# One decoder block on one core: the experts' rows packed in halves of 64, two halves per step

## The chip, the core and the metric

The kernel runs on one core of one Trainium2 chip. The metric is the device time of one launch in microseconds (us), the median over several executions. A profiled execution adds a trace, in which PE is TensorE's matmuls, PEld its weight loads, DVE is VectorE, ACT is ScalarE, POOL is GpSimd and SP is SyncE; a q behind a name (SPq) is that engine's instruction queue, where DMA issues and register work stand.

## The reference, cut to what matters

The block has a mixer (a projection, an SSD scan, attention, an output projection) and then a mixture of 32 experts. The change touches only the experts and the routing that prepares them. There are 1024 tokens of 1024 numbers, and each token goes to 2 experts of one group of 8:

```python
g_w, g_idx = lax.top_k(g_prob, 1)                 # one of 4 groups
e_w, e_idx = lax.top_k(e_prob, MOE_TOP_K)         # 2 of its 8 experts
w = g_w * e_w / sum(e_w)
gate = t @ w_gate[e]; up = t @ w_up[e]            # 1024 -> 256 each, float32
out += (silu(gate) * up * w) @ w_down[e]          # 256 -> 1024
```

So 2048 rows (token, expert) have to be computed. An expert's weights are three matrices of 1 MB, 3 MB in all. How many rows each expert gets follows from the reference and its inputs: for experts 0 to 31 it is 36, 106, 61, 55, 73, 31, 78, 86, 38, 33, 68, 47, 37, 26, 14, 63, 34, 45, 97, 50, 49, 133, 49, 97, 46, 191, 64, 121, 40, 69, 53, 58. Two experts have more than 128 rows. In pieces of at most 64 rows they are 45 pieces: 1 2 1 1 2 1 2 2 1 1 2 1 1 1 1 1 1 1 2 1 1 3 1 2 1 3 1 2 1 2 1 1.

## The kernel before

Everything is written by hand, with its own queue for each engine and counters (semaphores) between them. The work before the experts fills about 760 us: projection, scan, attention, output projection with residual, norm and router logits. Then a chain of small VectorE operations (lines 1497 to 1583) turns the router's choice into places: for each row of each tile the token that is to be gathered (`idx_i`) and the row to which the result goes (`dst_i`).

**Tiles.** Every expert has one tile of 128 rows, and rows beyond 128 go to extra tiles, two of them in straight code (`MORE`) and more in a branch that is taken only if needed. That makes 34 tiles (`TILES`), tile n for expert n, tiles 32 and 33 for the two experts over 128 rows. The last block of the program runs them; its functions are called `four` on each engine.

**One tile on TensorE**, in this order in its queue: `gate_up` of tile n (8 float32 matmuls with a stationary piece of `xg_T`, 128x128, and 512 moving columns, gate and up side by side; the profile counts a float32 matmul as two instructions, so 16), `tokens` of tile n+1 (8 transposes of the gathered rows `x_g`), `down` of tile n-1 (4 matmuls, 8 instructions) and `hidden_T` of tile n (2 transposes). ScalarE and VectorE copy the transposes into `xg_T` (`tx`), make SiLU(gate) and its product with up (`silu`, `gated`), and copy the results into `y_e` (`y_of`). GpSimd issues the gather of the rows and the scatter of the results (`gather`, `scatter_of`), after a copy of the index column (`idx_now`, `dst_now`).

**Weights.** `load_expert` on SyncE issues three DMAs of 1 MB into one of four slots (`RING` is 4). Tile n uses slot n mod 4. Experts 0 to 3 are loaded while the routing runs. From then on SyncE waits until `down` of the tile that last used the slot is done, and loads the next expert into it: the counter `dn_done` is raised by `down`.

**After the tiles** the results are read back from DRAM (`y_g`), weighted, summed, normed and stored; that part stays.

Of the kernel before, what the change touches and what calls it, by code (L numbers as in the profile page):

```python
# [7 lines left out]
F32 = mybir.dt.float32  # L8
# [6 lines left out]
P = 128  # L15
# [11 lines left out]
def hybrid_block(nc, x, c, positions, ada_w, ada_b, pre_norm_mix, post_norm_mix, pre_norm_ffn,  # L27
# [36 lines left out]
    with ctx:  # L64
# [18 lines left out]
        causal_b = keep("causal_b", [P, P], BF16)  # L83
        G1 = keep("G1", [P, D])
# [35 lines left out]
        XT = 16  # L120
        assert XT * (P + 1) > 2 * T - P
        NTILE = E + XT
# [4 lines left out]
        META = XT + 1  # L127
        meta_i = keep("meta_i", [P, META], I32)
# [80 lines left out]
        rt = [place(f"rt{i}", R_A + 81920 + 1024 * i, [P, NT, E]) for i in range(8)]  # L209
        oh1, oh2, lm, cand, both, rank, over, lm2 = rt  # L210
        oh1, oh2, lm, cand, both, rank, over, lm2 = (t[:, :, :] for t in rt)
# [3 lines left out]
        cmp = place("cmp", R_U + 3072, [P, XT, E])[:, :, :]  # L215
        cmp_n = place("cmp_n", R_U + 5120, [P, E, NT])[:, :, :]
# [5 lines left out]
        cnt, n_over, incl, base_t, lo128, dlt, zero32 = (tiny(f"tinyc{i}", 11 + i, [P, E])[:, :] for i in range(7))  # L222
# [5 lines left out]
        thr = tiny("thr", 23, [P, NT])[:, :]  # L228
        meta_f = tiny("meta_f", 24, [P, META])[:, :]
# [6 lines left out]
        W_OFF = [R_A + 32768, R_S, R_A, R_A + 57344]  # L236
        w_gu = [place(f"w_gu{i}", o, [P, 2, KC, FF]) for i, o in enumerate(W_OFF)]
        w_dn = [place(f"w_dn{i}", o + 16384, [P, FC, D]) for i, o in enumerate(W_OFF)]
        x_g = [place(f"x_g{i}", R_Z + 4096 * i, [P, D]) for i in range(2)]
        xg_T = [place(f"xg_T{i}", R_Z + 8192 + 4096 * i, [P, KC, P]) for i in range(2)]  # L240
        y_e = [place(f"y_e{i}", R_U + 4096 * i, [P, D]) for i in range(2)]
# [3 lines left out]
        idx_now = [place(f"idx_now{i}", R_A + 88064 + 32 * i, [P, 1], I32) for i in range(2)]  # L245
        dst_now = [place(f"dst_now{i}", R_A + 88128 + 32 * i, [P, 1], I32) for i in range(2)]
# [6 lines left out]
        w_diag = place("w_diag", R_U + 8192, [P, 2 * len(PE_TILES), P])  # L253
# [8 lines left out]
        def pe_sum(t):  # L262
# [15 lines left out]
            idx_read route_act wgu_loaded0 wgu_loaded1 wgu_loaded2 wgu_loaded3 wdn_loaded0 wdn_loaded1  # L278
            wdn_loaded2 wdn_loaded3             pool_step dve_step""".split()
# [3 lines left out]
            ye_stored1 v_gu0 v_gu1 v_dn0 v_dn1 v_xg0 v_xg1 v_idx v_tx v_txa v_txd v_gud v_silu v_hid v_th v_thr gathers_begun  # L283
            idx_step xg_loaded0 xg_loaded1 ya_scaled ysum_done ysum_sq o_scaled o_done o_stored yg_loaded0 yg_loaded1 yg_loaded2
            yg_loaded3 yg_loaded4 yg_loaded5 yg_loaded6 yg_loaded7 moe_stored w_diag ysum_pe dst_step v_stored v_down v_ya v_yd""".split()
# [992 lines left out]
        def load_expert(eng, e, r, gu, dn):  # L1278

            one = lambda v: v[bass.ds(e, 1), :, :, :].rearrange("a p k f -> (a p) k f")  # L1280
            eng.dma_start(w_gu[r][:, 0, :, :], one(wg_v)).then_inc(gu, 16)
            eng.dma_start(w_gu[r][:, 1, :, :], one(wu_v)).then_inc(gu, 16)
            eng.dma_start(w_dn[r][:, :, :], one(wd_v)).then_inc(dn, 16)

        EB = NG

        with nc.Block() as block:

            @block.sync
            def _(sp):  # L1290
# [10 lines left out]
                load_expert(sp, 0, 0, S["wgu_loaded0"], S["wdn_loaded0"])  # L1301
# [6 lines left out]
                load_expert(sp, 2, 2, S["wgu_loaded2"], S["wdn_loaded2"])  # L1308
                sp.wait_ge(S["x2_done"], NT)
                load_expert(sp, 3, 3, S["wgu_loaded3"], S["wdn_loaded3"])  # L1310
                sp.wait_ge(S["lg_done"], NT)
                load_expert(sp, 1, 1, S["wgu_loaded1"], S["wdn_loaded1"])
# [4 lines left out]
            @block.gpsimd  # L1317
            def _(pool):
                for t in range(NT):
                    inverse_root(pool, 5, t, S["yo_sq"], t + 1)  # L1320
                    inverse_root(pool, 6, t, S["x2_sq"], t + 1)

# [107 lines left out]
            def _(dve):  # L1430
# [98 lines left out]
                for j in range(2):  # L1529
                    dve.tensor_scalar(place_p[:, j:j + 1], tok_id[:, 0:1], 2.0, float(1 + j), ALU.mult, ALU.add)  # L1530
                dve.tensor_scalar(place_t, iota_row[:, 0:NT], 2.0 * P, None, ALU.mult)
                link(dve.tensor_scalar(thr, iota_row[:, 1:NT + 1], float(P), None, ALU.mult))
                dve.tensor_scalar(lo128, iota_row[:, 0:E], float(P), None, ALU.mult)
                dve.wait_ge(S["ranks_done"], 1)
                link(dve.tensor_copy(cnt, BANK[2][:, 0:E]))

                link(dve.tensor_tensor(cmp_n, cnt.unsqueeze(2).to_broadcast([P, E, NT]),
                                       thr.unsqueeze(1).to_broadcast([P, E, NT]), ALU.is_gt))
                link(dve.tensor_reduce(n_over, cmp_n, AX_X, ALU.add))
                link(dve.tensor_tensor_scan(incl, n_over, zero32, 0.0, ALU.add, ALU.add))  # L1540
                link(dve.tensor_tensor(base_t, incl, n_over, ALU.subtract))
                link(dve.tensor_scalar(base_t, base_t, float(E - 1), float(P), ALU.add, ALU.mult))
                link(dve.tensor_tensor(dlt, base_t, lo128, ALU.subtract))
                ex = lambda v: v.unsqueeze(1).to_broadcast([P, NT, E])
                rk = BANK[1][:, 0:NT * E].rearrange("p (t e) -> p t e", e=E)
                link(dve.tensor_scalar(over, rk, float(P), None, ALU.is_ge))
                link(dve.tensor_tensor(over, over, ex(dlt), ALU.mult))
                link(dve.tensor_tensor(rank, rk, over, ALU.add))
                link(dve.tensor_tensor(rank, rank, ex(lo128), ALU.add))
# [11 lines left out]
                for j in range(2):  # L1561
# [5 lines left out]
                    if j == 0:  # L1567
# [3 lines left out]
                link(dve.tensor_tensor(cmp, iota_row[:, 0:XT].unsqueeze(2).to_broadcast([P, XT, E]),  # L1571
                                       incl.unsqueeze(1).to_broadcast([P, XT, E]), ALU.is_ge))
                link(dve.tensor_reduce(meta_f[:, 0:XT], cmp, AX_X, ALU.add))
                link(dve.tensor_scalar(meta_f[:, 0:XT], meta_f[:, 0:XT], float(E - 1), None, ALU.min))
                link(dve.tensor_copy(meta_f[:, XT:], incl[:, E - 1:E]))
                dve.tensor_copy(meta_i[:, :], meta_f)
# [7 lines left out]
                dve.wait_ge(S["idx_read"], 1)  # L1584


        RING = 4
        assert E % RING == 0 and E > RING
        MORE = 2
        TILES = E + MORE  # L1590
        LATER_CREDIT = {"v_down": 2}

        with nc.Block() as block:  # L1593
            def rounds(eng, four):

                four(0, range(RING), True, False)
                with eng.Fori(1, E // RING - 1) as i:
                    four(i * RING, range(RING), False, False)
                four(E - RING, range(RING + MORE), False, True)

            def extra(eng, one):

                n_extra = eng.snap(eng.value_load(meta_i[0:1, XT:XT + 1], min_val=0, max_val=XT))
                with eng.If(n_extra > MORE):
                    with eng.Fori(MORE // 2, XT // 2) as i:
                        for u in range(2):
                            one(i, u)
# [3 lines left out]
            def _(sp):  # L1611
                def four(n0, us, first, last):
                    for u in us:
                        if first:
                            continue
# [358 lines left out]
```

## Time and profile before

| what | value |
|---|---|
| median of 3 executions | 1243.04 us (1242.4 to 1243.77) |
| profiled execution, its own time | 1242.94 us |
| its span, first to last instruction | 1240.3 us |
| granted TensorE clock, mean | 0.938 of full speed |
| PE busy in the span | 1061.1 us (86%) |
| from the first `gate_up` to the end of the last `down` | 800.91 to 1192.58 us |

The span is the time between the first and the last instruction of the trace; 2.6 us lie around it. A stretch of the trace is read by its granted clock first (1.00 is 2.4 GHz, 0.50 is 1.2 GHz), then by who waits for whom. "Idle before" in a row is the time in which an engine did nothing ahead of an instruction, with what ended it.

### The profile page before, as it was taken

Reading aid. Unit: us, or ns where it says so; the run is one execution under the profiler, and the core shown is the slowest. Engines: PE = TensorE matmul, PEld = TensorE weight load, DVE = VectorE, ACT = ScalarE, POOL = GpSimd, SP = SyncE. Lnnn points to the kernel's source line nnn. Section 1 sums busy time; section 2 is a strip of 40 time slices with the busy share of each in tenths; the row PEclk is TensorE's granted clock in tenths of the full one; section 3 lists DMA queues with packets and bytes.
Section 4 is the critical chain, followed back from the end, with each engine's and each line's share of the span. In section 5 each row is a group of like instructions: output and inputs, shape, how many; then the busy total and the mean of one; then the engine's idle time right before and its main releaser. Section 6 shows DMA issues by size and latency. Waiting matters only on the chain. (4 is left out here: it accounts for less than half of the span.)

```text
span 1240.3 us, 11686 instructions
## 1 busy us (share of the span) xinstructions
PE 1061.1 (86%) x4040; PEld 591.2 (48%) x4040; DVE 506.4 (41%) x825; ACT 260.0 (21%) x585; POOL 210.0 (17%) x324
## 2 busy tenths in 40 slices
PE   1499999996989999787699994399999999999954
PEld 1444444443455666587345553244445445444521
DVE  4543437345656555588143345511121112112217
ACT  1420001213444344233022211011111111111113
POOL 5100000223200000046210000112221221222114
PEclk9989999997999999898699996599999999999977
DMA  9763332000000000300401216238887878988537
GB/s 334 260 261 136 136 136 42 1 1 0 1 1 1 1 1 1 135 2 1 141 35 68 68 51 241 107 131 344 305 313 307 319 302 322 348 323 320 211 135 290
DMA packets 46355, 190.05 MB, mean 153 GB/s; under 512 B 17314, under 2 KB 18402, under 8 KB 29026
## 3 DMA queue, kind: packets, MB, share of 16 engines
q1 hardware_dynamic: 34596, 166.80, 35.8%
q0 software_dynamic: 10672, 18.45, 4.2%
q10 hardware_dynamic: 1040, 4.19, 0.9%
q8 instruction: 27, 0.44, 0.1%
q14 instruction: 20, 0.16, 0.0%
HBM read 182.07 MB, written 26.21 MB: 168 GB/s over the span
## 5 line engine op out<-in xcount | busy, mean ns | idle before, releaser
L1715 PE MATMUL PS<-w_gu,xg_T 128*128 128x512 f32 x544 | 241.5, 597 | 1.1 <-ACT xg_T L1800 1.1
L1715 PEld LDWEIGHTS PS<-w_gu,xg_T 128*128 128x128 f32 x544 | 101.8, 192 | 116.8 <-issue 115.2
L1726 PE MATMUL PS<-w_dn,hid_T 128*128 128x512 f32 x272 | 122.5, 593 | 0.9 <-DVE hid_T L1878 0.9
L1344 PE MATMUL PS<-w_out_sb,cat_T 128*128 128x512 f32 x256 | 113.5, 602 | 2.8 <-ACT cat_T L1400 2.8
L673 PE MATMUL PS<-hT,w_in_sb 128*128 128x512 f32 x256 | 112.2, 601 | 0.0
L1875 DVE TENSOR_TENSOR hid<-PS,hid_s 128x256 f32<-128x256 f32 x34 | 14.4, 425 | 224.2 <-ACT hid_s L1803 224.2
L361 POOL TENSOR_SCALAR rstd<-stat 128x1 f32<-128x1 f32 (+1 forms) x48 | 21.9, 456 | 408.1 <-ACT junk L468 206.3
L991 PE MATMUL PS<-kT,qT 96*128 96x512 f32 (+4 forms) x192 | 76.6, 509 | 3.0 <-ACT qT L782 3.0
L673 PEld LDWEIGHTS PS<-hT,w_in_sb 128*128 128x128 f32 x256 | 49.4, 193 | 62.1 <-issue 62.1
L1344 PEld LDWEIGHTS PS<-w_out_sb,cat_T 128*128 128x128 f32 x256 | 48.7, 193 | 62.0 <-issue 58.4
L876 DVE TENSOR_REDUCE row_max<-PS 128x1 f32<-128x1024 f32 (+7 forms) x64 | 48.2, 754 | 63.8 <-PE PS L993 63.7
L1726 PEld LDWEIGHTS PS<-w_dn,hid_T 128*128 128x128 f32 x272 | 49.2, 190 | 50.3 <-issue 49.3
L794 ACT ACTIVATE probs<-PS,row_max 128x1024 f32<-128x1024 f32 (+7 forms) x64 | 47.5, 742 | 97.8 <-DVE row_max L876 97.4
L1881 DVE COPY y_e<-PS 128x512 f32<-128x512 f32 x34 | 23.5, 692 | 95.6 <-PE PS L1726 95.6
L1803 ACT ACTIVATE hid_s<-PS 128x256 f32<-128x256 f32 x34 | 13.1, 385 | 222.5 <-PE PS L1715 222.5
L683 PE MATMUL PS<-w_in_sb,hT 128*128 128x512 f32 x128 | 56.2, 592 | 0.0
L1003 PE MATMUL PS<-ident,probs 128*128 128x128 f32 x288 | 43.4, 278 | 12.4 <-ACT probsT L802 6.9
L1657 POOL COPY dst_now<-dst_i 128x1 int32 (+1 forms) x34 | 6.2, 183 | 248.7 <-DVE y_e L1881 149.2
L1710 PEld LDWEIGHTS PS<-ident,x_g 128*128 128x128 f32 x272 | 35.9, 190 | 23.8 <-issue 15.9
L692 PE MATMUL PS<-w_in_sb,hT 128*128 128x424 f32 x128 | 46.9, 519 | 0.0
L635 PE MATMUL PS<-ident,xn 128*128 128x128 f32 x64 | 14.5, 404 | 36.7 <-DVE xn L490 36.7
L1003 PEld LDWEIGHTS PS<-ident,probs 128*128 128x128 f32 x288 | 30.9, 141 | 29.4 <-ACT probs L794 24.1
(318 smaller groups left out, 1441.1 us busy)
## 6 DMA issues: line engine op xcount, KB each, us to landing
w_gu<-in_w_gate_dram SPq DMA_DIRECT2D x34, 1024.0 KB, 4.9
w_gu<-in_w_up_dram SPq DMA_DIRECT2D x34, 1024.0 KB, 7.5
w_dn<-in_w_down_dram SPq DMA_DIRECT2D x34, 1024.0 KB, 10.6
ada_later<-in_ada_w_dram SPq DMA_DIRECT2D x16, 1024.0 KB, 4.9
ada_first<-in_ada_w_dram SPq DMA_DIRECT2D x8, 1024.0 KB, 12.6
y_g<-y_rows SPq DMA_DIRECT2D x8, 1024.0 KB, 11.8
x_in<-in_x_dram SPq DMA_DIRECT2D x8, 512.0 KB, 3.7
w_in_sb<-in_w_in_dram ACTq DMA_DIRECT2D x1, 4096.0 KB, 13.2
```

What stands on the lines that cost most here:

```text
L673: last = pe.matmul(BANK[4 + n % 4][:, :], w_in_sb[:, k, XC0 + ct * P:XC0 + (ct + 1) * P], hT[:, k, hh * HALF:(hh + 1) * HALF], start=(k == ...
L683: last = pe.matmul(BANK[t % 2][:, 0:IN_SSD], hT[:, k, t * P:(t + 1) * P], w_in_sb[:, k, 0:IN_SSD], start=(k == 0), stop=(k == KC - 1))
L692: last = pe.matmul(BANK[6 + t % 2][:, 0:REST], hT[:, k, t * P:(t + 1) * P], w_in_sb[:, k, XC1:], start=(k == 0), stop=(k == KC - 1))
L794: act.activation(probs[b][:, 0:n], PS[:, 2 * b:2 * b + 2, :].rearrange("p a n -> p (a n)")[:, 0:n], ACT.Exp, bias=row_max[:, b:b + 1], acc ...
L876: dve.tensor_reduce(row_max[:, b:b + 1], PS[:, 2 * b:2 * b + 2, :].rearrange("p a n -> p (a n)")[:, 0:n], AX_X, ALU.max, negate=True).then ...
L991: pe.matmul(BANK[2 * b + c0 // HALF][:, 0:c1 - c0], qT[h][0:depth(h), i * P:(i + 1) * P], kT[h][0:depth(h), c0:c1], start=True, stop=c1 < ...
L1003: last = pe.transpose(BANK[4 + j // 4][:, j % 4 * P:(j % 4 + 1) * P], probs[g % 2][:, j * P:(j + 1) * P], ident[:, :])
L1344: last = pe.matmul(BANK[2 + t % 2 * 2 + j], cat_T[t % 2][:, k, :], w_out_sb[:, k, j * HALF:(j + 1) * HALF], start=(k == 0), stop=(k == KC ...
L1710: last = pe.transpose(BANK[k // 4][:, k % 4 * P:(k % 4 + 1) * P], x_g[u][:, k::KC], ident[:, :])
L1715: last = pe.matmul(BANK[bank], xg_T[b][:, k, :], w_gu[r][:, :, k, :], start=(k == 0), stop=(k == KC - 1))
L1726: last = pe.matmul(BANK[5 + j], hid_T[b][:, k, :], w_dn[r][:, k, j * HALF:(j + 1) * HALF], start=(k == 0), stop=(k == FC - 1))
L1881: return dve.tensor_copy(y_e[b][:, HALF:], BANK[6])
```

## The change

Experts' rows are laid out in halves of 64 rows, one behind the other, each expert with at least one half. A step takes two consecutive halves, whatever experts they belong to: the first in rows 0 to 63, the second in rows 64 to 127. For each piece of the contraction TensorE gets two matmuls with 64 stationary columns, one for each half, which write PSUM partitions 0 to 63 and 64 to 127, and each has its own expert's weights as the moving operand. There are 23 steps in straight code (`STEPS`) and 9 more in a branch.

- The ring still has four slots of 3 MB. Where a step's experts lie is read from a small table (`pair_i`) into a register (`slot_of`). The first half's matmuls read the ring by that register.
- The second half's weights are copied first from the ring to a fixed place: `near_gu` (ScalarE its gate part, VectorE its up part, 128x2048 each) and `near_dn` (one 128x1024 each). There is one such buffer. ScalarE reads four more numbers from the table, how far each slot must have been loaded, and waits for the loads (`nearer`).
- SyncE reads from a table (`free_i`) after which step the slot of expert e-4 is free, waits for that `down`, and loads expert e. Nobody else waits for loads.
- The routing chain is shorter in front (no `cmp_n`, `over`, `cmp`), with 32 columns for 48, and a new chain of about 17 small VectorE operations makes the two tables at the start of the last block. The first two gathers are issued at the end of the block before it, and gathers and scatters take their indices without the copy.

The core of the diff; the functions of before that it removes are printed above:

```diff
-        XT = 16
-        NTILE = E + XT
+        HT = P // 2
+        RING = 4
+        NTILE = (E + 2 * T // HT) // 2
...
+        near_gu = place("near_gu", R_Z + 8192, [P, 2, KC * FF])
+        near_dn = [nc.alloc_sbuf_tensor_at("near_dn0", [P, D], F32, offset=SPENT + 8192), place("near_dn1", R_U + 8192, [P, D])]
...
+        STEPS = 23
...
             def _(sp):
+                sp.wait_ge(S["pairs_made"], 1)
+                for e in range(RING, E):
+                    r = e % RING
+                    used = sp.value_load(free_i[0:1, e - RING:e - RING + 1], min_val=1, max_val=NTILE)
+                    sp.wait_ge(S["dn_done"], used)
+                    load_expert(sp, e, r)
...
+                def gate_up(n, w):
...
+                    pe.wait_ge(S["near_gu_act"], n + 1)
+                    pe.wait_ge(S["near_gu_dve"], n + 1)
...
                     for k in range(KC):
+                        for u in range(2):
+                            rows_ = slice(u * HT, (u + 1) * HT)
+                            last = pe.matmul(BANK[2 + b][rows_, :], xg_T[b][:, k, rows_], gu[u][:, :, k, :],
+                                             start=(k == 0), stop=(k == KC - 1))
...
+                def run(lo, hi):
...
+                    for n in range(lo, hi):
+                        gate_up(n, now)
...
+                        if n + 1 < hi:
+                            now = pair(n + 1)
+                            tokens_T(n + 1)
+                        if n > lo:
+                            down(n - 1, was)
+                        hidden_T(n)
+                    down(hi - 1, before_)
...
+                def nearer(n):
+                    w = slot_of(act, 2 * n + 1)
+                    landed = [act.value_load(pair_i[2 * n + 1:2 * n + 2, 1 + r:2 + r], min_val=3 * 16, max_val=3 * 16 * E // RING)
+                              for r in range(RING)]
+                    for r in range(RING):
+                        act.wait_ge(S[f"w_loaded{r}"], landed[r])
+                    act.sem_inc(S["w_here"], 1)
+                    act.activation(near_gu[:, 0, :], w[:, 0 * KC * FF:1 * KC * FF], ACT.Copy).then_inc(S["near_gu_act"], 1)
...
+                        silu(n)
+                        if n + 1 < hi:
+                            nxt = nearer(n + 1)
+                            tx(n + 1)
+                        if n > lo:
+                            y_of(n - 1)
+                        nearer_down(n, now)
```

TensorE's queue before, one tile in the loop (line 1715 is `gate_up`, 1710 the transposes of the gathered rows, 1726 `down`, 1720 `hidden_T`):

```order
L1715 MATMUL PS<-w_gu_257,xg_T_267 128x512 x8
L1710 MATMUL PS<-ident,x_g_264 128x128 x8
L1726 MATMUL PS<-w_dn_260,hid_T_274 128x512 x4
L1720 MATMUL PS<-ident,hid_273 128x128 x2
L1715 MATMUL PS<-w_gu_258,xg_T_266 128x512 x8
```

TensorE's queue now, from the last matmuls of a `gate_up` (line 1678) to the first of the next one (1658 are the transposes of rows, 1703 `down`, 1687 `hidden_T`; TENSOR_LOAD is the register load, ISA register work):

```order
L1678 MATMUL PS<-ring,xg_T_263 64x512
L1678 MATMUL PS<-near_gu,xg_T_263 64x512
L1602 TENSOR_LOAD pair_i
L1602 ISA x2
L1658 MATMUL PS<-ident,x_g_262 128x128 x8
L1703 ISA
L1703 MATMUL PS<-ring,hid_T_275 64x512
L1703 MATMUL PS<-near_dn_268,hid_T_275 64x512
...
L1687 MATMUL PS<-ident,hid_272 128x128 x2
L1678 ISA
L1678 MATMUL PS<-ring,xg_T_264 64x512
L1678 MATMUL PS<-near_gu,xg_T_264 64x512
```

The order of the four groups is the one of before; each full matmul has become a pair of 64 columns with register work ahead, and `down` of step n-1 still stands between `gate_up` of n and of n+1.

ScalarE's queue before, one tile (1803 `silu`, 1800 `tx`, 1806 `y_of`):

```order
L1803 ACTIVATE hid_s_270<-PS 128x256
L1800 ACTIVATE xg_T_267<-PS 128x512
L1806 ACTIVATE y_e_269<-PS 128x512
```

ScalarE's queue now, one step from `silu` (1754) on. Row 1602 is the register with the slot, the four loads of 1765 say how far the slots must be loaded (the rows here are two of the four), 1770 waits for that and copies, 1746 is `tx`, 1761 `y_of`, 1776 the copy for `down`:

```order
L1754 ACTIVATE hid_s_271<-PS 128x256
L1602 TENSOR_LOAD pair_i
L1602 ISA x2
L1765 TENSOR_LOAD pair_i
L1765 ISA x2
L1765 TENSOR_LOAD pair_i
L1765 ISA x2
...
L1770 ISA
L1770 ACTIVATE near_gu<-ring 128x2048
L1746 ACTIVATE xg_T_264<-PS 128x512
L1761 ACTIVATE y_e_266<-PS 128x512
L1776 ISA
L1776 ACTIVATE near_dn_268<-ring 128x1024
```

Five register loads and the copy into `near_gu`, with its wait for the loads, have moved in between `silu` of a step and `tx` of the next one.

## Rows read from the trace of the kernel before

**Rows 1.** Page, granted clock and DMA share in 40 slices

```profile
PEclk9989999997999999898699996599999999999977
DMA  9763332000000000300401216238887878988537
```

**Rows 2.** Chain that ended last: start, length, engine, line, count

```profile
1029.08 6.87 PE PS L1715 x16
1036.83 3.44 PE PS L1726 x8
1040.49 6.87 PE PS L1715 x16
...
1188.87 3.71 PE PS L1726 x8
```

**Rows 3.** Waits on SyncE's queue, 800 to 1200 us: total, times, longest

```profile
SPq L1281 <- PE PS L1726: 296.8, 28, 30.9
```

**Rows 4.** Page, DMA issue of an expert's third matrix: median to landing

```profile
w_dn<-in_w_down_dram SPq DMA_DIRECT2D x34, 1024.0 KB, 10.6
```

**Rows 5.** Windows: busy per engine, granted clock, DMA share, GB/s

```profile
770.00:772.00 2.00, 0.00 (x0) 0.00 (x0) 1.86 (x5) 0.00 (x0) 0.00 (x0) 0.50 1.01 426
1000.00:1100.00 100.00, 100.00 (x301) 49.81 (x301) 19.07 (x36) 14.22 (x27) 20.17 (x34) 1.00 0.86 327
```

**Rows 6.** DMA queues, 790 to 1200 us: packets, MB, share of 16

```profile
q0 software_dynamic: 9792, 16.80, 11.0%
```

**Rows 7.** Timeline around a load of tiles: `down` end, SyncE's issues

```profile
1131.61 0.33 SPq L1281 DMA_DIRECT2D w_gu<-in_w_gate_dram  x1
1131.61 0.60 ACT L1806 ACTIVATE y_e<-PS 128x512 f32<-128x512 f32 x1 [2.84 <-PE PS L1726]
...
1143.03 0.60 ACT L1806 ACTIVATE y_e<-PS 128x512 f32<-128x512 f32 x1 [2.84 <-PE PS L1726]
...
1143.97 0.35 SPq L1281 DMA_DIRECT2D w_gu<-in_w_gate_dram  x1
...
1144.89 0.38 SPq L1283 DMA_DIRECT2D w_dn<-in_w_down_dram  x1
```

**Rows 8.** Timeline of TensorE in attention, 501 to 511 us

```profile
502.00 1.31 PE L1016 MATMUL PS<-probsT,v_sb 128*64 128x128 f32 x20
503.25 0.91 PE L991 MATMUL PS<-kT,qT 96*128 96x384 f32 x2
...
509.70 0.88 PE L1016 MATMUL PS<-probsT,v_sb 128*64 128x128 f32 x12
510.51 0.49 PE L991 MATMUL PS<-kT,qT 96*128 96x128 f32 x2
```

**Rows 9.** Groups by form: copies on ScalarE and VectorE, mean ns

```profile
L1800 ACT ACTIVATE xg_T<-PS 128x512 f32<-128x512 f32 x34 | 20.3, 598 | 43.4 <-PE PS L1710 43.4
L1421 ACT ACTIVATE junk<-x 128x1024 f32<-128x1024 f32 x8 | 8.5, 1058 | 28.6 <-DVE x L1478 28.6
L501 DVE TENSOR_SCALAR acc<-ada_later,c_act 128x2048 f32<-128x2048 f32 x2 | 2.6, 1278 | 0.0
```

**Rows 10.** Timeline, start of the expert stage

```profile
798.11 1.97 PE L1710 MATMUL PS<-ident,x_g 128*128 128x128 f32 x8 [7.67 <-DMA x_g<-h_rows,idx_now]
800.91 9.37 PE L1715 MATMUL PS<-w_gu,xg_T 128*128 128x512 f32 x16 [0.83 <-ACT xg_T L1800]
```

**Rows 11.** Windows of 1 us after it (clock is the third last)

```profile
804.00:805.00 1.00, 1.00 (x2) 0.34 (x1) 0.00 (x0) 0.00 (x0) 0.00 (x0) 0.50 0.36 147
806.00:807.00 1.00, 1.00 (x3) 0.40 (x3) 0.00 (x0) 0.00 (x0) 0.00 (x0) 1.00 0.00 0
```

**Rows 12.** Timeline of VectorE in the routing, then the first gather

```profile
779.09 0.42 DVE L1546 TENSOR_SCALAR rt<-PS 128x256 f32<-128x256 f32 x1
...
791.69 0.19 DVE L1583 TENSOR_SCALAR idx_i<-dst_i 128x48 int32<-128x48 int32 x1
...
793.87 1.19 POOL L1651 DMA_INDIRECT x_g<-h_rows,idx_now  x1 [0.98 <-POOL idx_now L1648]
```

More of the change, by code:

```diff
@@ L1583, in _, with steps, slot_of @@
                 dve.tensor_scalar(idx_i[:, :], dst_i[:, :], 1, None, ALU.logical_shift_right).then_inc(S["idx_read"], 1)
[L1584 to L1591, printed above, removed]
-        with nc.Block() as block:
[L1594 to L1607, printed above, removed]
+        with nc.Block() as block:
+            def steps(eng, run):
+                run(0, STEPS)
+                n_steps = eng.snap(eng.value_load(free_i[0:1, E - 1:E], min_val=1, max_val=NTILE))
+                with eng.If(n_steps > STEPS):
+                    run(STEPS, NTILE)
+            def slot_of(eng, m):
+                a = eng.value_load(pair_i[m:m + 1, 0:1], min_val=0, max_val=max(W_OFF) // (4 * UNIT))
+                return ring[:, bass.ds(a, SLOT), :].rearrange("p a b -> p (a b)")
@@ L1664, in scatter_of, with scatter @@
[L1664 to L1665 removed]
+                def scatter(n):
+                    b = n % 2
                     pool.wait_ge(S["ye_act"], n + 1)
                     pool.wait_ge(S["ye_dve"], n + 1)
[L1668 to L1680 removed]
@@ L1781, in _ @@
-                pe.wait_ge(S["ye_act"], TILES)
-                pe.wait_ge(S["ye_dve"], TILES)
-                extra(pe, one)
+                            for u in range(2):
+                                rows_ = slice(u * HT, (u + 1) * HT)
+                                last = pe.matmul(BANK[5 + j][rows_, :], hid_T[b][:, k, rows_],
+                                                 (near_dn[k] if u else far[:, k, :])[:, j * HALF:(j + 1) * HALF], start=(k == 0), stop=(k == FC - 1))
+                    last.then_inc(S["dn_done"], 1)
@@ new lines, in run @@
+                def run(lo, hi):
+                    tokens_T(lo)
+                    if lo == 0:
+                        pe.wait_ge(S["pairs_made"], 1)
+                    now = pair(lo)
+                    for n in range(lo, hi):
+                        gate_up(n, now)
+                        if n > lo:
+                            was = before_
+                        before_ = now
+                        if n + 1 < hi:
[5 more added lines that the diff above has]
+                    down(hi - 1, before_)
```

464 lines of the change are left out of this document (202 added, 262 removed).

## The prediction

> **What bounds the kernel now.** I read the granted clock first: full speed through the slices of the expert stage [rows 1], so matmul times there are at 2.4 GHz. Then the chain that ended last. From 801 to 1193 us it is TensorE alone, tile after tile: 6.87 us of `gate_up`, 3.44 of `down`, the transposes between, and the next `gate_up` starts 11.41 us after the last one [rows 2]. Nothing waits for weights: it is SyncE that waits for TensorE, 28 times, 296.8 us in all [rows 3]. That wait is what the reader should keep in mind, because it is the reserve. A slot is freed by `down` of tile n and needed again by `gate_up` of tile n+4, three tiles or 30 us later, and the load takes about 11.5. Last, the DMA share: 0.86 of 16 engines, 327 GB/s, in a stretch of full work [rows 5], so the transfers are close behind TensorE. 34 tiles of 11.41 are 388 us; with the cold start the stage takes 391.7.
>
> **The step on TensorE.** 45 halves make 23 steps in place of 34 tiles. Does a pair of 64-column matmuls cost one full matmul? The attention already does this: two heads write the two halves of the partitions in turn. 20 such instructions of 128 columns take 1.31 us and 12 take 0.88 [rows 8], so one more costs (1.31-0.88)/8 = 54 ns. A full matmul instruction of 512 columns costs 6.87/16 = 429 ns [rows 2], which is 107 ns for 128. The pair runs at full overlap, and I take a step's `gate_up` as 6.87 and `down` as 3.44. The bounds are 1.0 and 2.0 times that; the second is excluded by these rows except for what is new here, a register-addressed operand and register work ahead of each pair. I keep 1.3 as the upper end.
>
> At one place a rule and the rows have to be weighed. The next instructions after the 20 start at 503.25, 1.25 us after 502.00, where 20 x 54 ns is 1.08; after the 12 it is 0.81 against 0.65 [rows 8]. So a change between pairs and full matmuls seems to cost about 0.17 us. There are four in a step. Two of them (into the transposes, into `down`) lie before the release of a slot; in the steps that wait for weights, 11 by the count below, they are on the path: 11 x 0.35 = 4 us. The Trainium skill, TensorEngine Tiling (Array Packing), Key Properties, says that a change of tiling mode drains TensorE. It gives no time; by the rule alone all 92 changes would count, 92 x 0.17 = 16 us, an estimate, by these rows the sum has 4.
>
> **The chain on ScalarE.** After `gate_up` of n, ScalarE must do `silu`, five register loads, the copy into `near_gu` and `tx` before `gate_up` of n+1. A register load is in the trace only on SyncE: for tile 32's weights the first issue comes 0.94 us after the copy that starts at the same `down` end, without a load 0.00 [rows 7]. Five are 3.6 to 4.7 us; the lower bound is nothing, if they overlap. I take 3.75. The copy of 2048 from SBUF: 1058 ns for 1024 against 598 for 512 gives 1.92 us; VectorE's is 1.28 [rows 9] and starts with it, so ScalarE's ends later. With 0.2 to see the end of `gate_up`, 0.60 for `tx` and 0.3 of signals that is 6.8 us. TensorE covers 4.56 (its period of 11.43 less 6.87). A step that waits for nothing else takes 11.4 + 2.2 = **13.6 us**. With free loads the chain is 3.0, it is covered, and the step is 11.4.
>
> **The weights, which decide.** A slot is now free after `down` of the last step of expert e-4, and that `down` is one step late in the queue. 23 steps use 32 experts, often two new ones. Then four slots are two steps, and the second new expert of step n waits for `down` of n-2, which stands right before `gate_up` of n: no reserve is left of the 30 us. One load: 10.6 us from the third issue [rows 4], which is 0.92 behind the first [rows 7], so 11.5. Of it 3.15 MB at 426 GB/s are 7.4 [rows 5]; rows' gathers and scatters are 11.0% of 410 us over 34 tiles [rows 6], 1.3; 2.8 is latency. Now most of the scatter falls behind the wait (`y_of` stands behind it on ScalarE), so I leave 0.5 of it: 0.1 + 2.8 + 0.5 + 7.4 = 10.8 from `down` end to landed, then copy, `tx` and signals 2.9. `gate_up` of n starts 13.7 us after `down` of n-2, idle 13.5, which is 11.3 more than the 2.2 already counted.
>
> From the list of halves, which steps need an expert whose slot is freed how late:
>
> - after `down` of n-2, one load to wait for: steps 2, 3, 8, 9, 12, 13, 20 (experts 4, 5, 12, 14, 19, 21, 29). 7 x 11.3 = 79.
> - both new experts after `down` of n-2, one transfer behind the other: steps 10 and 11 (15, 16 and 17, 18). 2 x (11.3 + 7.4) = 37.
> - both after `down` of n-3: steps 6 and 15 (8, 9 and 22, 23). 21 us of loading and copying less a period of 13.6 and the 2.2: 2 x 5.0 = 10.
> - the other 11: none.
>
> **The clock.** The stage's first `gate_up` comes after idle time; it takes 9.37 us, at half clock until after 805 and full from 806 on [rows 10, 11]. That is 2.5 us over 6.87. In the new kernel TensorE is idle for 7 us or more ahead of 11 steps, and cold at steps 0 and 1: 13 x 2.5 = 32. Bounds: nothing, if the clock stays up, and 3.4 each if it rises later, counted from the first activity at 798.11 [rows 10].
>
> **Start and end.** The routing loses its longer ops (0.42 us for `over` and the like), about 3.4 us, and the gather goes out 2 us sooner, which is now 2.2 behind the table of indices [rows 12]. In return come the tables (17 small ops, under cover of the gather), and then five loads and the copy, 3.75 + 1.92. The two nearly cancel; the first `gate_up` stays at 800.9. The end has one `down` behind the last step as before; all behind it stays.
>
> **Sum.** 22 periods of 13.6 are 299.6; weights 79.1 + 37.4 + 10.0; clock 32.5; mode changes 4. From the first to the last `gate_up` 462.6. Then 6.87 + 0.9 + 3.44 + 0.2 + 1.2 + 3.44 = 16.1. The last `down` ends at 800.9 + 478.7 = 1279.6, where it was 1192.6: +87.0. The profiled execution took 1242.94, 0.1 under the median of the runs: **1330 us**.
>
> **The rivals.**
>
> - *Pairing pays (faster).* One mechanism: the loads keep ahead. Without any wait for weights and its cold starts the stage is 2.5 + 299.6 + 16.1 = 318 us, 74 less than now: 1169. For it speaks that 28 loads at 7.4 us are only 207 us of transfer. Against it speaks the order above: the transfer may not start. It decides from about 74 us of waiting on; I count 159 with the clock. To halve it, a load would have to land some 4 us after its release, at twice the 426 GB/s seen with all 16 engines busy [rows 5]. 5%.
> - *Cheap version of my own case.* Register loads overlap, the clock stays up: the steps of 13.6 become 11.4, but the waits that were shorter grow in their place (the loads don't come sooner), so only 17 us go with the loads, and 32 with the clock: 1281. 15% for something near it (below 1290).
> - *The pairs are dearer (slower still).* Register work and register addresses break the overlap in part: at 1.3 times, 0.3 x (6.87 + 3.44) = 3.1 us more in each of 23 steps, 71 in all, of which I take a fifth to replace idle time only, since some loads get a longer cover: 1330 + 57 = 1387. 12%. Without overlap at all, twice: about 1525. 2%.
> - *My case*, four slots and a late release, 1290 to 1365: 64%. A rest of 2% is for no change within 0.2%, which is about what a measurement of this kernel can tell from none.
>
> So: slower 0.93, same 0.02, faster 0.05. The range takes the cheap version on the low side and the 1.3 on the high side: 1283 to 1388. The likeliest case alone is 1290 to 1365.
>
> At the clock the Trainium skill, TensorE: Matmul & The Clock Gate, HAM oscillation, describes this shape, bursts of matmuls with a DMA wait between, each of which starts at half clock again. The one such start in this stage agrees (9.37 against 6.87); no row here shows a second one after a wait for weights, so the bound of nothing stays in the range.
>
> **What would show it.** In the changed kernel: 23 groups of `gate_up`, each about 6.9 us at full clock and 9.4 after a wait; if they take 9 at full clock, the pairs are dearer. Steps without a weight wait (4, 5, 7, 14, 16 to 19, 21, 22) start 13.6 us apart; if 11.4, the register loads are free. PE idle about 13.5 us ahead of steps 2, 3, 8, 9, 12, 13, 20 and 21 ahead of 10 and 11, ended by ScalarE's copy, which in turn waits for a DMA. DMA share in the stage falls from 0.86 to about 0.6, in full and empty stretches. SyncE's waits for `down` stay, but a wait for DMA appears on ScalarE's queue. Wrong I would be if slots are freed earlier than I read, if the clock never falls, or if a load lands in much less than 10.8 us.

## The result

The changed kernel takes 1323.14 us (median of 4 runs, 1319.70 to 1324.76) against 1243.17 for the kernel before in the same comparison: ratio 1.064, 95% interval 1.062 to 1.066. The profiled execution took 1319.70 us.

The page of the changed kernel, its 40 slices, shows where. The expert stage is now slices 25 to 39 (33 us each):

```profile
PE   1599999978899997876999725667754466687755
PEclk9899999988899998987999856778977777799887
DMA  9743412000000003003111071369655553867627
```

Beside [rows 1]: the clock no longer holds at 9 in the stage, TensorE is busy 4 to 8 tenths, and the DMA share swings between 3 and 9 from slice 26 to slice 38. All three fell at once, so no engine took TensorE's place as the bound. The stage as one window (busy time of PE, PEld, DVE, ACT, POOL, granted clock, DMA share, GB/s), of the changed kernel and then of the kernel before:

```profile
790.00:1280.00 490.00, 311.58 (x1334) 113.66 (x1334) 91.14 (x162) 98.53 (x116) 45.28 (x45) 0.81 0.55 216
```

```profile
800.00:1193.00 393.00, 390.53 (x1149) 193.18 (x1148) 71.89 (x136) 54.81 (x103) 79.12 (x130) 0.99 0.74 281
```

In [rows 5] the DMA share is 0.86 over 100 us; over the whole stage before it was 0.74, and it is 0.55 now.

The chain that ended last has become a relay between engines, where [rows 2] had TensorE alone (start, length, what). These are step 2's wait, step 2, and step 4 (L1678 is `gate_up`, L1703 `down`, L1289 and L1290 SyncE's issues, L1770 the near copy):

```profile
828.56 3.61 PE PS L1703 x16
832.19 0.34 SPq L1289
832.57 0.42 SPq L1290
833.04 8.85 DMA ring<-in_w_down_dram
...
842.39 1.53 issue
843.93 0.59 ACT xg_T L1746
844.51 0.13 issue
844.64 9.43 PE PS L1678 x32
...
886.57 7.09 PE PS L1678 x32
893.65 1.09 PE PS L1658 x8
894.74 3.61 PE PS L1703 x16
```

`down` ends at 832.17; at that moment SyncE may load; 9.7 us later (833.04 + 8.85) the weights are there, then copy and `tx`; `gate_up` begins 12.5 us after `down`. The waits of 790 to 1280 us (total, times, longest) say the same:

```profile
ACT near_gu L1770 <- DMA ring<-in_w_down_dram: 168.7, 14, 21.6
...
PE PS L1678 <- ACT xg_T L1746: 156.0, 22, 19.4
```

The second row names `tx` as releaser of TensorE, but `tx` (L1746) is a conversion of 0.6 us that stands in ScalarE's queue behind the near copy; the first row is the cause. From the first `gate_up` (803.87) to the last (1254.86) it is 451.0 us; the last `down` ends at 1271.0, where it was 1192.6.

### The profile page after: what moved, and what is told of

It is laid out like the page before. It is cut to its first block and busy times, and to the rows that moved or that the text cites. A ratio compares the mean times of both kernels' runs of the same rounds, so it can differ in the third digit from the quotient of the medians.

```text
span 1318.0 us, 12292 instructions
## 1 busy us (share of the span) xinstructions
PE 980.2 (74%) x4218; PEld 510.4 (39%) x4218; DVE 519.1 (39%) x835; ACT 303.4 (23%) x598; POOL 172.8 (13%) x234
## 5 line engine op out<-in xcount | busy, mean ns | idle before, releaser
L1678 PE MATMUL PS<-ring,xg_T 128*64 x368 | 193.2, 686 | 162.6 <-ACT xg_T L1746 156.0
L1678 PE MATMUL PS<-near_gu,xg_T 128*64 128x512 f32 x368 | 193.2, 686 | 0.0
L1678 PEld LDWEIGHTS PS<-ring,xg_T 128*64 128x64 f32 x368 | 55.7, 158 | 281.3 <-issue 281.3
L1878 DVE COPY near_gu<-ring 128x2048 f32 x23 | 28.2, 1228 | 190.2 <-ACTq L1769 190.2
L1770 ACT ACTIVATE near_gu<-ring 128x2048 f32 x23 | 44.0, 1911 | 202.1 <-DMA ring<-in_w_down_dram 168.7
L1703 PE MATMUL PS<-ring,hid_T 128*64 x184 | 83.8, 598 | 1.5 <-DVE hid_T L1866 1.5
L1703 PE MATMUL PS<-near_dn,hid_T 128*64 128x512 f32 x184 | 83.8, 599 | 0.0
L1859 DVE TENSOR_TENSOR hid<-PS,hid_s 128x256 f32<-128x256 f32 x23 | 9.8, 425 | 188.0 <-ACT hid_s L1754 188.0
L1631 POOL DMA_INDIRECT y_rows<-y_e,dst_i x23 | 23.1, 1003 | 409.3 <-ACT y_e L1761 394.8
L1678 PEld LDWEIGHTS PS<-near_gu,xg_T 128*64 128x64 f32 x368 | 55.7, 158 | 0.0
## 6 DMA issues: line engine op xcount, KB each, us to landing
ada_first<-in_ada_w_dram SPq DMA_DIRECT2D x8, 1024.0 KB, 12.2
```

The lines of the kernel that those rows point to most:

```text
L1678: last = pe.matmul(BANK[2 + b][rows_, :], xg_T[b][:, k, rows_], gu[u][:, :, k, :], start=(k == 0), stop=(k == KC - 1))
L1703: last = pe.matmul(BANK[5 + j][rows_, :], hid_T[b][:, k, rows_], (near_dn[k] if u else far[:, k, :])[:, j * HALF:(j + 1) * HALF], start=(k ...
L1770: act.activation(near_gu[:, 0, :], w[:, 0 * KC * FF:1 * KC * FF], ACT.Copy).then_inc(S["near_gu_act"], 1)
L1878: dve.tensor_copy(near_gu[:, 1, :], w[:, 1 * KC * FF:2 * KC * FF]).then_inc(S["near_gu_dve"], 1)
```

## The experiments

Twelve kernels, each timed against the kernel before. The first four ask what the time went to: the moment at which a slot is freed, the bytes, the price of a step, or the clock.

**e1, loads of an eighth.** In `load_expert`, for experts from 4 on:

```
+ kc, dc = (KC, D) if e < RING else (1, D // 8)
- eng.dma_start(w_gu[r][:, 0, :, :], wg_v[e])
+ eng.dma_start(w_gu[r][:, 0, 0:kc, :], wg_v[e][:, 0:kc, :])
```

and `up` and `down` alike.

> From expert 4 on, each weight load brings only its first eighth (one of 8 column groups of gate and of up, 128 of 1024 columns of down); the rest of a slot keeps an older expert's weights, so the output is not the reference's. Order, waits and all engine work stay. Late-release theory (a slot is freed right before it is needed, and a whole load then stands on the path): the waits for weights nearly vanish, steps start 12.6 us apart, 22 x 12.6 + 2.5 of cold start + 16 = 296 us from the first gate_up, about 170 less than now: 1150 us. Rival, the price of the step itself (pairs, near copies, register loads): the steps stay as long as they are and the time stays above 1290. A mixture would lie between. The clock should stay at its upper level but for the first steps.

Measured: 1225.36 us (ratio 0.987, interval 0.985 to 0.988). 98 less than the changed kernel, but 75 over what was expected: the expectation was wrong. The chain of e1, the wait of step 9 (L1679 is `gate_up`, L1704 `down`):

```profile
942.50 3.61 PE PS L1704 x16
946.12 0.34 SPq L1290
946.50 0.43 SPq L1291
946.98 2.80 DMA ring<-in_w_down_dram
...
950.39 1.47 issue
951.86 0.59 ACT xg_T L1747
...
952.57 9.47 PE PS L1679 x32
```

The relay is whole, only its DMA piece went from 8.8 to 2.8. Nine of the 11 steps still wait (5.9 us for one load, 8.6 for two, at steps 10 and 11) and start cold; steps 6 and 15, whose loads start one `down` sooner, don't. So the bytes are a little over half of the price (98 of the 168 us between the changed kernel and e8 below, which has neither the bytes nor the late release); issue, latency, copy, `tx` and the clock are the rest, and they are paid by the order of the program however small a load is.

**e2, a warm clock.** In `gate_up`, ahead of its waits:

```
+ if n in WARM:
+     pe.wait_ge(S["w_diag"], 1)
+     for _ in range(WARM[n]):
+         pe.matmul(BANK[7], ident[:, :], w_diag[:, 0:4, :], start=True, stop=True)
```

> Ahead of the waits of gate_up at the 11 steps that wait for weights, TensorE gets full 128x512 float32 matmuls into an unused PSUM bank: 12 of them at steps 2, 3, 8, 9, 12, 13, 20, 20 at steps 10 and 11, 7 at step 6 and 9 at step 15, sized (0.86 us each at full clock) to end before the weights land. Clock theory: gate_up after a wait takes 7.1 us in place of 9.4 to 9.9, and the time falls by 11 x 2.5 = 27 us, to 1296; idle ahead of gate_up shrinks by the matmuls, the starts of gate_up less the preceding down stay 12 us. Rival, the slow gate_up after a wait has another cause (the first use of new weights, a busy SBUF under the landing DMA): no change, 1323. If the matmuls overrun the wait, the time falls less or rises, and gate_up's idle is then 0.

Measured: 1301.55 us (ratio 1.048, interval 1.045 to 1.051), 22 less than the changed kernel where 27 was expected. Timeline of its TensorE at step 3 (start, length, idle before in brackets):

```profile
857.91 10.47 PE L1672 MATMUL PS<-w_diag,ident 128*128 128x512 f32 x24
870.25 0.64 PE L1684 MATMUL PS<-ring,xg_T 128*64 x1 [1.87 <-ACT xg_T L1752]
```

`gate_up` starts 12.2 us after the last real matmul (12.0 in the changed kernel) and takes 7.08 in place of 9.81; so it is in 8 of the 11 steps. Steps 10, 11 and 15, where the matmuls ended 2.2 to 3.6 us early, took 8.8, and so did two steps that had been warm (5 and 19, behind 2.6 and 1.7 us of idle), while others stayed warm behind 1.7 to 2.3. The slow `gate_up` after a wait is the clock: the granted clock of step 3 is 1.00 from 870 to 872 us, against 0.50 in the changed kernel, and at 7.08 nothing is left over.

**e3, the slots freed in two parts.** On SyncE:

```
- for e in range(RING, E):
-     used = value_load(free_i[e - RING])
-     sp.wait_ge(S["dn_done"], used)
-     load_expert(sp, e, e % RING)
+ for e in range(RING, E + 2):
+     for part, m in (("gu", e), ("dn", e - 2)):      # where RING <= m < E
+         used = value_load(free_i[m - RING])
+         sp.wait_ge(S[part + "_done"], used)
+         load_gu(m) if part == "gu" else load_dn(m)
```

with a landing semaphore for each part and slot; VectorE loads four more registers per step and waits for the `down` part.

> The slots are freed in two parts. SyncE loads gate and up of expert e as soon as the gate_up of the last step of expert e-4 is done, and down of expert e-2 behind it, as soon as down of the last step of expert e-6 is done; each part has its own semaphores, the down part's landing is waited for by VectorE (four register loads more, ahead of its wait for down) and passed on. All bytes are still moved. Late-release theory: gate_up(n-2) ends 18 us before gate_up(n) starts in a 12.6 us step, a load of 2.1 MB lands 8 us after its release, two after 13, so nearly all waits go: 1150 to 1175 us, first to last gate_up about 280 to 300 us. Rival, bandwidth: the transfers can't be had faster, the waits move to the new semaphores, the time stays above 1280 with the DMA share near 1. Rival, step cost: above 1280 with no weight waits.

Measured: 1162.49 us, ratio 0.936, interval 0.935 to 0.938. All bytes are moved, no engine does less, and 161 us are gone: the kernel is now faster than before. `gate_up` starts 12.63 to 12.96 us apart in 17 of the 22 periods; apart from the cold start at steps 0 and 1, TensorE is kept waiting for weights at steps 10 and 11 alone (4.3 and 3.1 us). Its DMA in windows, full clock beside it:

```profile
805.00:1000.00 195.00, 177.58 (x818) 66.31 (x816) 52.58 (x81) 59.54 (x69) 25.23 (x25) 0.97 0.90 364
```

0.90 in this stretch, and 0.81 from 790 to 1115 us, the whole stage, where it had been 0.55: the capacity was there, the permission to use it was not.

**e4, halves one after the other.**

```
- for k in range(KC):
-     for u in range(2):
+ for u in range(2):
+     for k in range(KC):
```

> In gate_up alone the loop over the two halves is put outside that over k: 8 matmuls of the lower half, then 8 of the upper, in place of turns. Same instructions, same operands. Overlap theory (a pair costs one matmul because the two halves of the array work at once, which needs turns): gate_up takes 13.7 us at full clock in place of 7.1; 23 x 6.6 = 152 us, of which up to 11 x 6.6 = 73 replace idle time: 1400 to 1460 us. Rival, the queue looks far enough ahead or the halves need no turns: 1323, gate_up at 7.1. Rival, the pair is bound by something else that both halves share (moving data at 64 columns costs half): unchanged as well.

Measured: 1421.27 us, ratio 1.145, interval 1.143 to 1.147. Step 4's `gate_up` on TensorE:

```profile
907.83 5.79 PE L1678 MATMUL PS<-ring,xg_T 128*64 x13 [0.46 <-ACT xg_T L1746]
913.03 0.64 PE L1678 MATMUL PS<-near_gu,xg_T 128*64 128x512 f32 x1
913.46 0.59 PE L1678 MATMUL PS<-ring,xg_T 128*64 x1
```

Each half alone goes on at 0.43 us per record, no faster than a pair in turns (in the changed kernel both halves of step 4 start at 886.57 and then every 0.43). So a pair is two matmuls in the time of one, and it needs the turns. It took 12.28 us and not 13.7, because the upper half begins 3 records before the lower one ends.

The next four take the step apart.

**e5, register loads ahead of silu**, alone, and **e7**, the same on top of e3:

```
+ ahead = table(n + 1)          # slot and 4 landed counts of step n+1
  silu(n)
- nxt = nearer(n + 1)
+ nxt = nearer(n + 1, *ahead)
```

> The changed kernel, with the five register loads of ScalarE for step n+1 placed ahead of its silu of step n, where it waits for TensorE anyway; the waits for the weights stay where they were. The profile has the five loads at 2.65 us between silu and the near copy. Chain theory: steps that wait for no weights fall from 12.65 us to the length of TensorE's own work, 7.1 + 1.1 + 3.6 + 0.2, or of the shortened chain, about 11.9; steps that wait for weights don't change, for the loads are over long before. Of 22 periods the 11 without a wait gain 0.8 each, but where the next wait hangs on a down that now comes earlier it gains too: 1310 to 1316 (from 1323). Rival, the order makes no difference because loads and copy hide elsewhere: 1323.

> Both in one: slots freed in two parts, and ScalarE's register loads ahead of silu. In the split version the later half of the steps is bound by ScalarE's chain (silu, loads 2.65, copy 1.9, tx 0.6: 12.65 us a step, TensorE idle 0.5 to 0.9), the earlier half by the transfers at 420 GB/s. Chain theory: the later steps fall to 11.9 us, and the time from 1162 to 1152 to 1156. If the transfers are the bound of the whole stage (28 loads of 7.4 us and the rows' traffic are 207 + 45 = 252 us at least), the gain is smaller, 1158 to 1162.

Measured: e5 1324.07 us (ratio 1.063, 1.061 to 1.066): nothing, below the 7 to 13 expected. e7 1151.70 (ratio 0.926, 0.925 to 0.928): 11 less than e3. The same edit is worth 0 in one kernel and 11 us in the other. In e5 the freer steps run ahead (step 1 starts 12.71 after step 0, in place of 14.88) and meet the next wait for weights earlier; steps 5, 17, 19 and 22 now wait 1.9 to 3.6 us and run at 8.6 to 9.9, cold. What e7 removes is seen in the chain of e3 (L1776 is the table's loads):

```profile
994.83 7.11 PE PS L1689 x32
1001.96 0.30 ACT hid_s L1765
1002.52 0.58 ACTq L1776
1003.35 0.29 ACTq L1776
1003.90 0.29 ACTq L1776
1004.44 0.29 ACTq L1776
1005.39 1.69 issue
1007.08 0.58 ACT xg_T L1757
1007.79 7.11 PE PS L1689 x32
```

From the end of `gate_up` to the next it is ScalarE, 5.8 us (the 1.69 called issue lies in the copy into `near_gu`). In e7 most periods are 12.13, which is TensorE's own work (7.02, 1.10, 3.58 and 0.44 in its chain).

**e6, the gathers back in the expert block**: `gather(pool, 0)` and `gather(pool, 1)` are taken from the end of the preceding block and stand first in `run`.

> The changed kernel, with the first two gathers moved back from the end of the preceding block into the first loop of GpSimd in the expert block, as the kernel before has them. In the changed kernel TensorE and VectorE enter the block 7.5 us after the indices are there. Theory: the end of a block waits for GpSimd's two indirect transfers to be issued; without them the block starts some 6 us sooner, the first gather lands at about 798 at the latest, the tables are made beside it, and the first gate_up comes at 798 to 801 in place of 803.9: 1318 to 1321. Rival, the gap is the block's end itself (instruction fetch of the longer program): first gate_up unchanged or later by the gather's landing, 1323 to 1326.

Measured: 1321.63 us (ratio 1.062, 1.060 to 1.064), just above the 1318 to 1321 expected, and the interval doesn't separate it from the changed kernel. The start itself is separated. VectorE writes the indices, the block ends, its first table follows; the changed kernel, then e6:

```profile
787.64 0.18 DVE L1588 TENSOR_SCALAR idx_i<-dst_i 128x32 int32<-128x32 int32 x1
795.31 0.18 DVE L1822 TENSOR_SCALAR free_i<-incl 128x32 int32<-128x32 f32 x1 [7.49 <-PEq L1303]
```

```profile
788.07 0.18 DVE L1584 TENSOR_SCALAR idx_i<-dst_i 128x32 int32<-128x32 int32 x1
788.57 0.18 DVE L1820 TENSOR_SCALAR free_i<-incl 128x32 int32<-128x32 f32 x1 [0.32 <-PEq L1303]
```

With two gathers at the end of a block, VectorE's first work in the next one comes 7.5 us after its last (TensorE starts at the same 795.31); without them, 0.3. In all ten kernels here with the gathers at the end of the block, the changed one included, it is 7.3 to 8.2, and 0.3 in the three without (e6, e11, e12). The first `gate_up` comes at 801.65 (798 to 801 expected) in place of 803.87. From there to the last one it is 458.6 us, against 451.0; steps 17 and 19 run cold here, and this profiled execution is the slowest of its four, the changed kernel's the fastest, so how much of it the earlier start causes isn't shown.

**e8, e3 with loads of an eighth.**

> The split version, and each load from expert 4 on brings its first eighth alone, as in e1, so the output is not the reference's. It gives the time with neither a late release nor bytes to wait for. With the late release an eighth of the bytes still gave 1225. Theory: the release decides, so here every step is 12.65 us long: first to last gate_up 22 x 12.65 + 2.5 = 281 us, 1143 to 1150. Rival, an eighth of the bytes cost the same here as there (small transfers are slow to land whatever the release): above 1200.

Measured: 1154.73 us (ratio 0.928, 0.926 to 0.930). Every period from the third on is 12.6 to 13.0, and from first to last `gate_up` it is 282.8 us, 281 expected (the stage began 4 us later than e3's in this execution). The time is 5 us over the 1143 to 1150 expected. An eighth of the bytes gains 8 us here and 98 in the late-release kernel. Steps 10 and 11 wait 0.46 us like all others, where e3 had 4.3 and 3.1: those two waits were for bytes.

The last four turn the release around from two sides, and try the best version.

**e9, two parts, late release.** e3 with one thing undone:

```
- sp.wait_ge(S[part + "_done"], used)      # and the down part two experts behind
+ sp.wait_ge(S["dn_done"], used)           # and the down part right behind
```

> Control for e3: its semaphores, its tables, its landing waits in two parts, but SyncE waits for down (dn_done) ahead of both parts, as in the changed kernel, and issues the down part right behind gate and up. Only the moment of release is undone. Release theory: the waits come back. The near copy now waits for two thirds of a load, some 2.5 us less than in the changed kernel in each of 11 steps, and a second load behind it less too: 1285 to 1300, against 1323 and 1162. Rival, what helped in e3 was the finer landing wait: below 1200.

Measured: 1287.28 us, ratio 1.035, interval 1.033 to 1.036. 125 us come back with the moment of release. (The `down` part's place in the queue is undone with it; it can delay only a second load, by the 1.05 MB of one matrix, an estimate of 2.5 us at the 426 GB/s of [rows 5], as at steps 6, 10, 11 and 15.) The finer landing wait is worth the other 36: steps wait 9.6 us in place of 12.0.

**e10, the release moved in another way.** On TensorE, with ScalarE and VectorE in the same order:

```
  tokens_T(n + 1)
- if n > lo: down(n - 1, was)
  hidden_T(n)
+ down(n, before_)
```

> The release moved in another way: loads and semaphores of the changed kernel, but down(n) stands right behind hidden_T(n), ahead of gate_up(n+1), where the changed kernel has it one gate_up later; the copies and conversions on ScalarE and VectorE follow that order. A slot is then free one gate_up (7 us) sooner. The price: TensorE waits in each step for the gated product and its transposed copy, so that a step without weight waits takes 13.0 us in place of 12.65. Release theory: from down(n-2) to the earliest gate_up(n) are 13.0 us, a load and its copies need 12.4 to 13.7, so 7 steps wait under 1 us and stay warm, steps 10 and 11 wait 7 to 8 for the second transfer, steps 6 and 15 not at all: first to last gate_up about 310 us, last down at 1127 to 1135, total 1175 to 1185. Rival, the step's own price or the loads' bytes: above 1280.

Measured: 1177.67 us, ratio 0.948, interval 0.946 to 0.950. No new semaphore, no new table, no byte less: `down` moved ahead of one `gate_up`, with the calls of ScalarE and VectorE put in the same order, is worth 145 us. Its chain has what it costs, the copy that TensorE now waits for (L1859), and what a step without a weight wait looks like:

```profile
897.58 6.96 PE PS L1678 x32
904.54 1.09 PE PS L1658 x8
905.63 0.37 PE PS L1687 x2
...
906.02 0.44 DVE hid_T L1859
...
906.59 3.67 PE PS L1703 x16
...
910.28 0.33 SPq L1289
```

The step is 12.66 us and not the 13.0 expected, since most of this copy lies in what had been idle anyway. The last row begins one of the waits that are left: this `down` is step 7's, its load queues behind two others, and TensorE is idle 5.6 us ahead of step 9, and 8.8 two steps on. From first to last `gate_up` it is 312.6 us, 310 expected, but not with the waits where they were expected: step 10 waits 1.2 and not 7 to 8, step 9 5.6, and step 13 2.9 with a cold start.

**e11 and e12, the best version.** e11 is e7 with e6's gathers; e12 adds small matmuls ahead of `gate_up` at steps 0, 10 and 11 (`pe.matmul(BANK[7][:, 0:P], ident, ident)`, 20, 30 and 16 times).

> e7 with the first two gathers in the expert block, as in e6. The block then starts 7 us sooner behind the indices and the first gate_up comes some 2.5 us sooner, and now nothing that waits for loads swallows it: 1148 to 1150, against 1152. Rival, the spread from run to run hides it: 1151 to 1153.

> e11 with small float32 matmuls of 128 columns into an unused PSUM bank ahead of gate_up in the three steps that still start cold: 20 at step 0, 30 at step 10, 16 at step 11. In e7 these gate_ups took 9.36, 8.41 and 8.45 us against 7.09. Clock theory: 5 us less, 1143 to 1146, if the matmuls reach far enough into the waits (idle of 5.6, 6.3 and 3.5 us). Rival, at step 0 they run at half clock and end before the clock has risen, then only the 2.7 us of steps 10 and 11 are gained: 1146 to 1148.

Measured over five rounds: e11 1148.26 us (ratio 0.924, interval 0.922 to 0.926), e12 1148.35 (0.923, 0.922 to 0.924). e11 beats both kernels, by 96 us the one before and by 175 the changed one; against e7 (0.926, 0.925 to 0.928) the intervals overlap. In e12 step 0 takes 7.09 in place of 8.92, and nothing is gained. The clock (third last) in e12 and then in e11, the same two stretches:

```profile
812.00:814.00 2.00, 1.42 (x4) 0.45 (x6) 0.95 (x2) 0.66 (x2) 0.64 (x1) 0.69 0.99 414
814.00:816.00 2.00, 2.00 (x8) 0.57 (x6) 0.46 (x2) 0.43 (x1) 0.00 (x0) 0.50 0.99 416
```

```profile
812.00:814.00 2.00, 0.23 (x2) 0.03 (x1) 1.83 (x2) 1.50 (x2) 1.36 (x1) 1.00 0.89 319
814.00:816.00 2.00, 1.95 (x10) 0.80 (x12) 1.03 (x2) 1.06 (x1) 0.11 (x1) 1.00 1.01 418
```

After a short idle ahead of step 1 (1.8 us) e12's clock falls, and step 1 takes 8.78; e11 keeps the upper level through a like idle and takes 7.08. At step 10 `gate_up` takes 7.09 in place of 9.64, but step 11 waits for a load and starts when it did (947.02 and 947.12); step 11 had been warm in e11 already. The expected 2.7 to 5 us were wrong for both places. That the earlier warming made step 1 cold isn't shown by one execution of each.

## Why the prediction was right, and where its sizes were off

The mechanism was right, and so was its count: the steps that wait long for weights are 2, 3, 6, 8 to 13, 15 and 20, the eleven of the list. e3, e9 and e10 show the cause: free the same slots sooner, in two different ways, and the waits go; put the release back, with all else of e3, and they return. So the step of the reasoning that the forecast hung on, a slot freed right before it is needed, holds. One reading behind it was wrong: in the kernel before, `down` of tile n ends right before `gate_up` of n+2, so the slot is needed two tiles later, 22.8 us, and not "three tiles or 30 us"; no term was made from it. The terms one by one:

- **The pair as one matmul.** `gate_up` 7.09 us and `down` 3.61 at full clock, for 6.87 and 3.44 in the sum. The transposes went from 0.9 to 1.09. The records inside a `gate_up` follow each other at 0.43 us in both kernels, so the excess lies where the groups meet. In e7, where TensorE alone bounds the step, it is 12.13 us against 11.41: 0.72 for four changes between pairs and full matmuls, 0.18 each. The 0.17 read from [rows 8] was the right size, and it is paid in every step that TensorE bounds. The 1.3 and 2.0 of the dearer pairs are excluded, and e4 shows on what it hangs. The Trainium skill, TensorEngine Tiling (Array Packing), Key Properties, says that a change of tiling mode drains TensorE. The 0.18 agrees with that; its size is from these rows alone.
- **ScalarE's chain.** The step without a wait is 12.65 us, not 13.6: the term was over-sized. The five loads take 2.65 us, 0.53 apart, where 0.94 each was read from [rows 7], which had another engine's load with a wait behind it, and 3.75 taken. The copies take 1.91 and 1.23 us, as priced (the rows given for the first make 1.98, not 1.92); `silu`'s 0.30 had been left out of the chain. The direction "nothing if they overlap" is closed: e7 shows 11 us for them. Over 22 periods the term was 278 and not 300.
- **A late load.** Predicted 10.8 from `down` end to landed and 2.9 to `gate_up`; measured 9.7 and 2.8, idle 12.0 and not 13.5; two loads 19.4 and not 21; steps 6 and 15 8.0 and 10.4 and not 7.2. As the steps are shorter they cover less of a wait, and four small waits that the list did not have (steps 5, 17, 19, 22: 1.5, 2.9, 2.2, 1.2) join. Taken over the 0.46 that every step has, the waits behind step 1 add up to 142 us, and 127 was predicted.
- **The clock.** 13 cold `gate_up`s were predicted at 2.5 us each, and 13 there are: 8.45 to 10.03 us against 7.09, 30 us in all for 32 (e2 gives back 22 of them). The window in which step 3's begins and the one in which it nears its end (clock third last), as in [rows 10, 11]:

```profile
871.00:873.00 2.00, 1.83 (x6) 0.62 (x8) 0.98 (x3) 1.46 (x3) 0.68 (x1) 0.50 1.03 434
...
877.00:879.00 2.00, 2.00 (x12) 0.67 (x10) 0.00 (x0) 0.00 (x0) 0.00 (x0) 1.00 0.21 78
```

The Trainium skill, TensorE: Matmul & The Clock Gate, HAM oscillation, describes bursts of matmuls with a DMA wait between, each of which starts at half clock again. The trace agrees at all 11 steps behind a long wait for weights; the other two cold starts, steps 0 and 1, stand behind other waits.
- **The start.** Wrong in its working, though only by 3.0 us (803.87 for 800.9). "Under cover of the gather" was false: the tables and the transposes both waited for the block to begin, 7.5 us after the indices, which no term had; the gathers' transfers were over by then (no DMA traffic from 794.6 on, the engines start at 795.31). That the loads were cheaper hid a part.
- **Sum.** 451.0 us from first to last `gate_up`, for 462.6; last `down` +78.4, for +87.0; 1323 for 1330. The too long step (-22 us) and the too small waits (+15) cancel in part. So the sum is nearer than its terms, in part by luck. It is no luck alone: a wait for a load counts from a fixed release, so what is taken from a step that ends in a wait goes to the wait, as e5 shows.
- **The rivals.** "Pairing pays" was priced at 1169 and said to be kept off by the order alone. The order taken away, it is 1162 (e3). That rival's price was right, and so was its condition. "To halve it, a load would have to land in 4 us" was too narrow a way to look: e9 takes off 36 us by waiting for two thirds of the load, and e10 145 by an order of lines.

The delay around steps 10 and 11 that e3 and e11 keep, 10 to 11 us over regular periods with their cold starts in, is the transfers' own: from 928 to 955 us of e3 the DMA share is 1.01 at 421 GB/s, and with an eighth of the bytes (e8) it is gone. What stays open is whether the same loads, spread otherwise, would avoid it, and what decides whether the clock holds through a short idle.

## What to carry to other kernels

When a loop is made shorter by doing more per step, count a ring of buffers anew in steps, not in buffers: four slots were two tiles of reserve (22.8 us, for a load of 11.5) and became none. Look which instruction frees a buffer and what stands between it and the next use; to free it in parts, or to move that instruction ahead of one long piece of work, was worth 145 to 161 us here, where the transfer's bytes, the register loads and the clock were worth 0 to 98. And price a small edit only in the kernel whose bound it touches: register loads gave nothing while steps waited for weights, and 11 us after.

## What the runs showed of the hardware that was not expected

- Two indirect transfers issued by GpSimd at the end of a block hold VectorE and TensorE there: 7.3 to 8.2 us from VectorE's last instruction to its next in ten kernels, against 0.3 in the three without them (e6, e11, e12). In the changed kernel the issues end at 791.21, the transfers' traffic at 794.6, and the engines start at 795.31; the traces don't say which of the two they wait for.
- Two 64-column float32 matmuls on the two halves run wholly at once, also with a moving operand addressed by register, 0.43 us per record of a pair; queued one half after the other they do not, but for 3 records where the two meet (e4).
- A register load from SBUF takes ScalarE 0.53 us with its register work (0.28 of it the load), five in a row 2.65.
- The length of a short idle alone doesn't tell whether the clock falls. It fell behind 1.8 us ahead of step 1 in e12 and behind 1.7 ahead of step 19 in e2; it held through 1.8 in e11, 2.3 ahead of step 22 in e2, and 2.9 ahead of step 17 in the changed kernel.
